# Feed-forward up projection: high products of both slabs before the low products of both

## The reference

```python
# first block: causal_dwconv is a 3-tap convolution over the tokens, per channel
h = causal_dwconv(hn @ w_ffn_up[l], conv_w[l], conv_b[l])
h_gate, h_val = h[..., :D_FF], h[..., D_FF:]
x = x + (jax.nn.silu(h_gate) * h_val) @ w_ffn_down[l]
# second block
g, u = jnp.split(x @ w_in, 2, axis=-1)
return (jax.nn.silu(g) * u) @ w_out
```

## Time and profile before

| | us |
|---|---|
| median of 3 runs | 719.13 |
| lowest, highest | 719.09, 720.16 |
| the profiled execution | 719.61 |
| its span, first to last instruction | 717.9 |
| PE matmul busy | 712.9 (99%) |
| DVE busy | 558.8 (78%) |
| ACT busy | 376.2 (52%) |
| POOL busy | 49.8 (7%) |
| granted TensorE clock, mean | 0.999 of 2.4 GHz |

### The profile page before, as it was taken

The page is one execution under the profiler, slowest core; times in us unless marked ns, Lnnn a source line. Parts: engine busy times, 40 slices in busy tenths (PEclk is TensorE's granted clock), DMA queues, the critical chain, the costliest instruction groups (busy, mean ns, idle before and its releaser), DMA issues.

```text
span 717.9 us, 11338 instructions
## 1 busy us (share of the span) xinstructions
PE 712.9 (99%) x4394; PEld 631.8 (88%) x4394; DVE 558.8 (78%) x673; ACT 376.2 (52%) x463; POOL 49.8 (7%) x61
## 2 busy tenths in 40 slices
PE   9999999999999999999999999999999999999998
PEld 8998887888888888899999888998988888888886
DVE  4979868899998889987578877987788666566673
ACT  7646466765555455565556554544456434433341
POOL 1255100001110000021000000000000000000000
PEclk9999999999999999999999999999999999999999
DMA  8765324356555455446335445455626555554521
GB/s 350 295 202 189 125 110 165 117 194 230 176 199 211 175 185 203 148 148 253 120 124 178 169 175 177 143 201 185 214 80 246 223 176 181 195 207 177 180 115 58
DMA packets 19610, 129.18 MB, mean 180 GB/s; under 512 B 2289, under 2 KB 2545, under 8 KB 4977
## 3 DMA queue, kind: packets, MB, share of 16 engines
q1 hardware_dynamic: 19424, 128.51, 49.4%
q10 hardware_dynamic: 144, 0.10, 0.1%
HBM read 126.50 MB, written 1.05 MB: 178 GB/s over the span
## 4 chain that ended last, share of the span: by engine, by line
PE 99%; DMA 1%; ACT 0%; DVE 0%; issue 0%
PE ps L1878 21%; PE ps L1854 14%; PE ps L1855 14%; PE ps L1856 14%; PE ps L1886 11%; PE ps L1898 8%; PE ps L1903 4%; PE ps L2092 1%; PE ps L2115 1%; PE ps L2122 1%; PE ps L1826 1%; PE ps L1923 1%; PE ps L1939 1%; PE ps L1811 1%; DMA h<-in_x 1%; PE ps L1956 1%
## 5 line engine op out<-in xcount | busy, mean ns | idle before, releaser
L651 ACT ACTIVATE hiw<-raw 128x2048 fp32r<-128x2048 f32 x116 | 221.8, 1914 | 199.9 <-PE ps L1886 100.0
L1107 DVE TENSOR_TENSOR low<-raw,hiw 128x2048 fp32r<-128x2048 f32 x116 | 269.3, 2324 | 63.7 <-ACT hiw L651 63.2
L1878 PE MATMUL ps<-xx,hiw 128*128 128x512 f32 x656 | 156.2, 390 | 0.0
L1878 PEld LDWEIGHTS ps<-xx,hiw 128*128 128x128 f32 x656 | 121.5, 188 | 24.4
L1886 PEld LDWEIGHTS ps<-xx,low 128*128 128x128 f32 x656 | 83.9, 191 | 3.0
L1886 PE MATMUL ps<-xx,low 128*128 128x256 f32 x656 | 85.2, 283 | 0.0
L1854 PE MATMUL ps<-hiw,yhi 128*128 128x512 f32 x208 | 81.7, 393 | 0.0
L1855 PE MATMUL ps<-low,yhi 128*128 128x512 f32 x208 | 81.2, 390 | 0.0
L1856 PE MATMUL ps<-hiw,ylo 128*128 128x512 f32 x208 | 81.0, 389 | 0.0
L1854 PE MATMUL ps<-xx,hiw 128*128 128x256 f32 x240 | 68.7, 286 | 0.0
L1437 DVE TENSOR_REDUCE arena<-ps 128x512 f32<-128x1024 f32 x41 | 50.1, 1221 | 23.3 <-PE ps L1886 23.2
(11 more groups left out here) (283 smaller groups left out, 962.5 us busy)
## 6 DMA issues: line engine op xcount, KB each, us to landing
raw<-in_slabs SPq DMA_DIRECT2D x116, 1024.0 KB, 4.8
vec<-in_vec SPq DMA_DIRECT2D x1, 1258.5 KB, 7.5
cst<-in_cst SPq DMA_DIRECT2D x1, 1220.0 KB, 13.4
h<-in_x SPq DMA_DIRECT2D x2, 512.0 KB, 4.3
raw<-in_slabs SPq DMA_DIRECT2D x2, 512.0 KB, 6.7
arena<-arena SPq DMA_DIRECT2D x16, 64.0 KB, 4.6
out<-h SPq DMA_DIRECT2D x1, 512.0 KB, 2.7
out<-h SPq DMA_DIRECT2D x2, 256.0 KB, 2.0
```

The costliest lines, as they stand in the source:

```text
L651: act.activation(hiw[:, n % SPLIT, :], raw[:, n % RAW, :], ACT.Copy).then_inc(hi_made, 1)
L1107: dve.tensor_tensor(low[:, n % SPLIT, :], raw[:, n % RAW, :], hiw[:, n % SPLIT, :].bitcast(F32), ALU.subtract).then_inc(lo_made, 1)
L1878: pe.matmul(banks[:, c, :], hi[:, kt, cc_], xx[:, kt].rearrange("p a b -> p (a b)"), start=kt == 0, stop=False)
```

## The change

In steps 1 to 8 of both feed-forward parts PE now does high(g), high(v), low(g), low(v), down. The function for one slab is split into `wide_high` and `wide_low`; steps 0, 9 and 10 keep their order.

```diff
-            def feature_major_wide(banks, n, low_made, middle=None):
+            def wide_high(banks, n):
...
-                pe.wait_ge(*low_made)
-                if middle is not None:
-                    middle()
+
+            def wide_low(banks, n):
...
             def ffn_up(k, f, i=None, parts=2):
                 n = AT[(k, f"g{f}")]
-                for j in range(parts):
-                    pe.wait_ge(*hidden_free(k, f, j, i, done=False))
-                    halves_made = n + j + 1 if i is None else n + j + 1 + 6 * i
-                    pe.wait_ge(hi_made, halves_made)
-                    up_made = feature_major_wide(wide_hidden(j), n + j, (lo_made, halves_made))
-                    up_made.then_inc(hidden_full(k, f, j)[0], 1)
+                made = [n + j + 1 if i is None else n + j + 1 + 6 * i for j in range(parts)]
+                both = [tuple(range(parts))] if f < FF - 2 else [(j,) for j in range(parts)]
+                for slabs in both:
+                    for j in slabs:
+                        pe.wait_ge(*hidden_free(k, f, j, i, done=False))
+                        pe.wait_ge(hi_made, made[j])
+                        wide_high(wide_hidden(j), n + j)
+                    for j in slabs:
+                        pe.wait_ge(lo_made, made[j])
+                        wide_low(wide_hidden(j), n + j).then_inc(hidden_full(k, f, j)[0], 1)
```

More of the change, by code:

```diff
@@ L1870, in feature_major @@
                 return mm
-            def feature_major_wide(banks, n, low_made, middle=None):
-                hi, lo = slab_views(n, KT)
+            def wide_high(banks, n):
+                hi, _ = slab_views(n, KT)
                 for c in range(2):
@@ L1879, in feature_major_wide @@
                                   start=kt == 0, stop=False)
-                pe.wait_ge(*low_made)
-                if middle is not None:
-                    middle()
+            def wide_low(banks, n):
+                _, lo = slab_views(n, KT)
                 for c in range(2):
@@ L2260, in ffn_up_first @@
                 pe.wait_ge(hi_made, n + 1)
-                feature_major_wide(wide_hidden(1), n, (lo_made, n + 1), back).then_inc(hidden_full(k, 0, 1)[0], 1)
+                wide_high(wide_hidden(1), n)
+                pe.wait_ge(lo_made, n + 1)
+                back()
+                wide_low(wide_hidden(1), n).then_inc(hidden_full(k, 0, 1)[0], 1)
             def ffn_down(k, f, i=None):
```

## The result

| | before | after |
|---|---|---|
| median, us (13 runs each, side by side) | 719.76 | 721.05 |
| lowest to highest, us | 718.83 to 720.16 | 720.37 to 721.90 |
| ratio after / before | | 1.0022 (95% interval 1.0015 to 1.0029) |
| the profiled execution, us | 719.61 | 720.62 |
| its span, us | 717.9 | 718.9 |

The change makes the kernel 0.22% slower. That is 1.6 us, with 1.1 to 2.1 as the ends of the interval; the two medians differ by 1.29. Wall times of single executions scatter by up to 1.5 us, and part of the span lies in front of the feed-forward parts: the first up product of the first block starts at 135.07 before and at 134.52 after, and nothing of the change is ahead of it. It is 579.63 us before and 581.18 after: **+1.55 us**.

The account below looks back on a forecast made before the run. PE, 99% busy, was taken as the bound from end to end. Seams -0.3, the down(10) stall +1.55 and step 1 +0.25 gave +1.5 us on 719.13: 720.6 us, ends 720.1 to 721.2, range 719.0 to 721.9.

Parts of the forecast that it names:

- the two cases on whose edge it lay: Whole kernel: slower means over 720.57 us, chance 0.53; same means from 717.7 to 720.57, chance 0.44.
- PE bounds everything: Whole kernel: PE is busy 99% of the span, so every hole opened on PE goes into the time in full.
- Seams: Steps 1 to 8, both parts: one high group no longer follows a low group, 0.02 us saved per step, -0.3 us.
- DVE's chain in step 8: First block: g's later low products delay DVE's queue, so low d8 starts at 289.03, 1.93 us later than before.
- The stall and its hand-over: First half of down(10), first block: PE waits 1.37 us for `y_low(10)` plus 0.18 hand-over, +1.55 us.
- Step 1: First block: high(v1) waits for the sum of v0, short by 0.08 plus hand-over, +0.25 us (0.1 to 0.4).
- POOL's stall at down(2): Rival, steps 2 to 4: POOL's 3.99 us delays `y_low`, PE waits 1.2 plus hand-over, 721.9 us; chance 0.10.
- the 2.9 that I gave the other loop steps: Loop steps: `y_low(f)` ends about 24.7 after the step's start, down(f) comes at 27.6, a margin of 2.9 us.
- The lateness dying out: Rival, before down(10): DVE's lateness falls from 1.93 to under 0.4, no hole opens, 719.1 us; chance 0.12.

## Why the prediction was right

It gave 720.6 us and +1.5, with slower by over 0.2% as the likelier of the two cases on whose edge it lay; measured were 721.05, a ratio of 1.0022, and +1.55 in the trace. Which side of the edge it fell on is not settled by the times, whose interval (0.15 to 0.29%) has 0.2% inside it. The kernel before stood 0.63 higher in the runs side by side than the 719.13 that the 720.6 was built on; that is nearly all of the miss in microseconds. That the sum came within 0.05 is in part luck, as two terms were off by 0.03 and 0.06 in opposite directions. Point by point:

- **PE bounds everything, so each hole counts in full and nothing gives it back.** Right. Nothing gives the 1.58 us back: behind the first block PE is 1.70 us later than before, and 1.55 at the last matmul. The 0.15 between are the seams of the second block.
- **Seams.** -0.31 against -0.3, and the steps of the second block are 16.55 too. The rule of the Trainium skill quoted in the prediction (TensorE: Matmul & The Clock Gate, Back-to-back issue gap) would have given 0. It is stated for isolated matmuls, and these follow each other without a pause; the rows disagree with it by 0.02 us a step.
- **DVE's chain in step 8.** The forecast had low d8 at 289.03 on the clock of before, 31.8 after the step's start. It started at 288.59, the step at 256.80: 31.79. The rows in between, in the timeline of DVE after, follow at the distances taken from the earlier trace rows:

```profile
280.37 0.69 DVE L1500 TENSOR_TENSOR ylo<-arena,yhi 128x512 fp32r<-128x512 f32 x1
280.97 1.21 DVE L1555 TENSOR_REDUCE st<-arena 128x8 f32<-128x1024 f32 x1
...
282.30 1.22 DVE L1437 TENSOR_REDUCE arena<-ps 128x512 f32<-128x1024 f32 x1
...
288.59 2.28 DVE L1107 TENSOR_TENSOR low<-raw,hiw 128x2048 fp32r<-128x2048 f32 x1
...
304.63 0.68 DVE L1500 TENSOR_TENSOR ylo<-arena,yhi 128x512 fp32r<-128x512 f32 x1
```

- **The stall and its hand-over.** The bare lateness was 1.37 in the forecast and is 1.34 in the trace: `y_low(10)` ends at 305.31, and without the wait PE would have started at 303.74 + 0.23 = 303.97. The hand-over was put at 0.18, and what stands in its place is 0.24: 0.07 from the end of `y_low(10)` to PE's start at 305.38, and 0.17 in the distances behind the hole, a loss that the forecast did not know. Together 1.58.
- **Step 1.** 0.27 against 0.25. Its place in the profile was wrong: I looked for it in the waits of PE at L1878, where it doesn't stand; it is with the weight loads.
- **POOL's stall at down(2) did not come.** The gate of step 2 starts at 178.64 and `y_low(2)` ends at 183.94, 5.30 later (5.31 forecast). down(2) starts at 185.12, with a margin of 1.2. But the 2.9 that I gave the other loop steps doesn't hold for steps 3 (1.3) and 4 (2.2), where POOL held `y_low` too. In the trace of before it had held the slab's low part there, and I took only step 2's row. It had no effect on the time, as the margins were enough.
- **The lateness dying out did not come.** The gains moved early, from behind step 8, and the two extra products in step 9 show that DVE's queue from there to down(10) carries its lateness through: 1.34 for 1.33, and 0.82 for the 0.88 expected. In step 9's new order it does break off, as the idle 1.66 shows, but in a way that costs more.

What went wrong was in the expectations of the experiments: the lower clock was not thought of, the hole with the gains early in step 9's new order was given 1.3 us too short, the stall at down(3) was given 0.4 too long, and the sum of v0 was moved ahead without pricing what it makes late at down(0).

## What to carry to other kernels

Where one engine is busy 99% of the time, a reordering of its work can save little, here only seams, and its price is paid in the queues behind it: look for the operation that now becomes ready later, follow the in-order queue from it to the first point where the bound engine needs its result, and compare the lateness with the margin there. The same reordering can be free in fifteen places and cost everything in the sixteenth, where the margin is a third of the lateness, so it should be switched by place. Before mending such a place by moving work, check that the engine which does the moved work does not idle between the new spot and the needed result; if it does, the gain is lost there.

## What the runs showed of the hardware

- **The clock.** After a wait of PE of 2.3 us amid dense work, TensorE went from 2.4 to 1.2 GHz for about 3 us in one traced execution and not in another of the same program; it came 1.3 us after PE had resumed, and cost 1.60 us. By the mean granted clock it came in five of ten executions with a hole of 2.5 us and in none of 26 with one of 1.4 us. Where it comes, the hole's 2.5 us turn into 4.1 (2.50 + 1.60), and the restart adds 0.17.
- **Restart.** Behind every hole read above the distance from the first product to the second is 329 to 341 ns instead of 227, be the hole 2.5 us or 0.07. Where there is hardly a hole at all it is 295 to 308 (down(0) with the sum first; d9 at 301.4 with step 9 in the new order). At down(10) of the changed kernel nine of the next ten distances are a few ns longer. That is 0.17 us on top of the idle time, and in no wait of the profile.
- **Who blocks whom.** POOL's operations after the gates of steps 3 and 4 took 1.90 and 2.80 us before and 3.87 and 4.70 after, with the same work. Before, DVE's low part of a slab (2.28 alone) stretched to 3.92 and 3.02 beside them; after, it keeps 2.28 and `y_low` (0.68 alone) stretches to 2.38 and 1.52. POOL's timeline after, then DVE's before and after in step 3:

```profile
195.94 3.87 POOL L624 TENSOR_TENSOR arena<-vec 128x1024 f32<-128x1024 f32 x1 [12.55 <-DVE arena L1485]
```

```profile
193.14 3.92 DVE L1107 TENSOR_TENSOR low<-raw,hiw 128x2048 fp32r<-128x2048 f32 x1 [0.20 <-ACT hiw L651]
```

```profile
195.77 2.28 DVE L1107 TENSOR_TENSOR low<-raw,hiw 128x2048 fp32r<-128x2048 f32 x1
197.97 2.38 DVE L1500 TENSOR_TENSOR ylo<-arena,yhi 128x512 fp32r<-128x512 f32 x1
```

  In step 3 DVE loses 1.64 us before and 1.70 after, whichever of its operations comes second. What changed is who started first. The low part waited 0.20 for ACT before, and POOL had begun at 193.01; after, DVE didn't wait and began at 195.77, and POOL's 3.87 contains the 2 us for which it was held. The Trainium skill (SBUF — State Buffer, SBUF: two separate sides) says that the one that starts first keeps the shared port pair for its whole instruction and the other blocks; the rows of steps 2 and 3 agree. Those of step 4 do not. POOL's and DVE's timelines before:

```profile
209.47 2.80 POOL L626 TENSOR_SCALAR arena<-arena 128x1024 f32<-128x1024 f32 x1 [14.56 <-DVE arena L1485]
```

```profile
209.63 3.02 DVE L1107 TENSOR_TENSOR low<-raw,hiw 128x2048 fp32r<-128x2048 f32 x1 [0.33 <-ACT hiw L651]
```

  POOL starts first and ends at 212.27. A low part of 2.28 that was held to there would end at 214.55; it ends at 212.65, 0.74 late. So the two ran side by side for most of POOL's 2.80. After, `y_low(4)` likewise loses 0.84 and ends at 216.06, while POOL works on to 217.28. Why this operation of POOL's (one input) holds DVE only briefly is not shown. An operation's length in such rows is not its work.
